# Turning activations by VectorE squares and DMAs instead of TensorE, in a two-layer hybrid decoder on one core

## What is computed

```
layer 0:  h += 0.5*SwiGLU(rms(h));  h += S5(rms(h));    h += 0.5*SwiGLU(rms(h))
          k, v = rms(h) @ w_kv
layer 1:  h += 0.5*SwiGLU(rms(h));  h += attn(rms(h));  h += 0.5*SwiGLU(rms(h))
out = rms(h)
swiglu(x) = (silu(x @ w_in[:, :F]) * (x @ w_in[:, F:])) @ w_out          # F = 2816
S5: 64 groups of 16 channels, 64 complex states each, a linear scan over time,
    then gelu, then (z @ w_glu[:, :1024]) * sigmoid(z @ w_glu[:, 1024:])
attn: 16 heads of 64, causal in the one block of 256 tokens, with a distance penalty
```

## Time and profile before

| | us |
|---|---|
| median of 3 runs | 972.12 (972.08 to 974.28) |
| profiled execution, its own time | 969.86 |
| its span, first to last instruction | 967.7 |
| TensorE busy | 955.9 |
| VectorE, ScalarE, GpSimd busy | 597.8, 499.8, 189.5 |

### The profile page before, as it was taken

How to read it: one execution, slowest core, us unless ns; L and a number is a source line. 1 busy time by engine, 2 the same in 40 slices (tenths; PEclk the granted TensorE clock), 3 DMA queues, 4 the chain that set the end, 5 groups by cost and what they waited for, 6 DMA issues and landing times.

```text
span 967.7 us, 15102 instructions
## 1 busy us (share of the span) xinstructions
PE 955.9 (99%) x6110; PEld 790.2 (82%) x6110; DVE 597.8 (62%) x744; ACT 499.8 (52%) x711; POOL 189.5 (20%) x235
## 2 busy tenths in 40 slices
PE   9999999999999999999999999999999999999997
PEld 7888888788788888888888888888888888888886
DVE  5565779889765554656555555555557555656544
ACT  7554544576555454545544454554458454545441
POOL 4899999800000000000000000000060000000000
PEclk9999999999999999999999999999999999999999
DMA  9766555520455655565566666656651366555551
GB/s 347 269 184 197 181 174 174 175 69 5 142 187 193 194 178 194 184 208 183 166 198 196 193 177 196 191 177 195 188 182 45 111 198 193 186 187 192 179 169 43
DMA packets 47557, 169.35 MB, mean 175 GB/s; under 512 B 5505, under 2 KB 5505, under 8 KB 47489
## 3 DMA queue, kind: packets, MB, share of 16 engines
q1 hardware_dynamic: 47056, 167.79, 54.5%
q10 hardware_dynamic: 432, 0.61, 0.2%
HBM read 167.33 MB, written 1.05 MB: 174 GB/s over the span
## 4 chain that ended last, share of the span: by engine, by line
PE 88%; DVE 8%; issue 2%; ACT 1%; DMA 1%; SPq 0%; POOLq 0%; POOL 0%; DVEq 0%; ACTq 0%
PE ps L1252 85%; DVE w_lo L931 2%; PE ps L1257 2%; DVE scan L1158 1%; DVE tmp L1087 1%; PE ps L1284 1%; DMA raw<-in_in 1%; DVE rot_b L1165 1%; DVE rot_a L1145 1%; DVE rot_b L1147 1%; ACT w_hi L652 0%; DVE rot_in L1154 0%; DVE states L1172 0%; PE ps L1297 0%; ACT pr L881 0%
## 5 line engine op out<-in xcount | busy, mean ns | idle before, releaser
L931 DVE TENSOR_TENSOR w_lo<-raw,w_hi 128x1024 fp32r<-128x1024 f32 x311 | 399.7, 1289 | 307.0 <-ACT w_hi L652 305.7
L652 ACT ACTIVATE w_hi<-raw 128x1024 fp32r<-128x1024 f32 x311 | 328.4, 1059 | 305.9 <-PE ps L1252 303.2
L1252 PE MATMUL ps<-w_hi,x_hi 128*128 128x512 f32 x896 | 352.4, 393 | 0.9 <-DVE w_lo L931 0.6
L1252 PE MATMUL ps<-w_hi,x_lo 128*128 128x512 f32 x896 | 349.3, 390 | 0.0
L1252 PE MATMUL ps<-w_lo,x_hi 128*128 128x512 f32 x896 | 349.2, 390 | 0.0
L1252 PEld LDWEIGHTS ps<-w_hi,x_hi 128*128 128x128 f32 x896 | 168.4, 188 | 37.2 <-DVE w_lo L931 1.4
L1252 PEld LDWEIGHTS ps<-w_hi,x_lo 128*128 128x128 f32 x896 | 168.3, 188 | 35.2
L1252 PEld LDWEIGHTS ps<-w_lo,x_hi 128*128 128x128 f32 x896 | 168.5, 188 | 34.0
L1252 PE MATMUL ps<-w_hi,hid_hi 128*128 128x512 f32 x352 | 138.1, 392 | 1.0 <-DVE w_lo L931 1.0
L1252 PE MATMUL ps<-w_lo,hid_hi 128*128 128x512 f32 x352 | 137.2, 390 | 0.0
L1252 PE MATMUL ps<-w_hi,hid_lo 128*128 128x512 f32 x352 | 137.2, 390 | 0.0
(11 more groups left out here) (151 smaller groups left out, 599.6 us busy)
## 6 DMA issues: line engine op xcount, KB each, us to landing
raw<-in_in SPq DMA_DIRECT2D x175, 512.0 KB, 4.3
raw<-in_out SPq DMA_DIRECT2D x88, 512.0 KB, 3.4
raw<-in_glu SPq DMA_DIRECT2D x16, 512.0 KB, 4.3
raw<-in_k SPq DMA_DIRECT2D x8, 512.0 KB, 4.4
raw<-in_v SPq DMA_DIRECT2D x8, 512.0 KB, 4.1
raw<-in_q SPq DMA_DIRECT2D x8, 512.0 KB, 4.4
raw<-in_o SPq DMA_DIRECT2D x8, 512.0 KB, 4.0
xt<-in_xt SPq DMA_DIRECT2D x4, 256.0 KB, 5.6
```

The source lines that it names most:

```text
L652: act.activation(w_hi[:, gu % WS, :], raw[:, gu % RAW, :], ACT.Copy)\
L931: dve.tensor_tensor(w_lo[:, gu % WS, :], raw[:, gu % RAW, :], w_hi[:, gu % WS, :].bitcast(F32), ALU.subtract)\
L1252: return pe.matmul(o, w, x, start=start, stop=stop, skip_group_check=True)
```

## The change

Three kinds of data are no longer turned by TensorE: the gated blocks of all four feed-forwards, the blocks of k and q, and those parts of h that are listed in `SHEETS` (GLU 0 to 2, and the first block of the outputs 4 and 8). `BY_ROWS` lists the nine parts of h that TensorE still turns.

In place of it VectorE transposes every square of 32 by 32 in itself (`dve.transpose`), gated blocks in place in `prod`, k, q and h into a new tile `sheet`. The squares then have to change places: square (q, c), of token group q and channel group c, goes to partitions 32c. SyncE does that with 16 DMAs per block, SBUF to SBUF, one for each (q, c), in pieces of 32 floats. They go to `hid_lo`, `x_lo`, `k_sb` or `q_sb`. ScalarE makes the high part of what has landed, and VectorE subtracts in place.

The moves stand in SyncE's queue behind the load of a fixed unit (8 units, `MOVE_BEHIND`, behind the block's end). Gated blocks are copied by ScalarE in unit 1 of the block after next, and finished by VectorE in unit 2. Parts of h from a sheet are read in unit 3 of the next block (GLU), or units 4 and 5 (outputs). q's scale moves into the norm's factor, one more small GpSimd instruction. There is one sheet, so a drain of k or q waits until the sheet before has been moved; `scores` waits for the move of its q block.

```diff
-BATCH = 4
-BATCHES = (0, 4, 8)
+SLOTS = 4
+SHEETS = [(2, 0), (2, 1), (2, 2), (4, 0), (5, 0), (5, 1), (8, 0), (9, 0), (9, 1)]
+BY_ROWS = [(2, 3), (4, 2), (4, 3), (8, 2), (8, 3), (10, 0), (10, 1), (10, 2), (10, 3)]
+MOVED = 16 * QS * QS
+MOVE_BEHIND = 8
...
 def high_behind(p, phases, b, j):
-    if p.name == "in" and b in BATCHES[1:] and j >= 2:
+    if p.name == "in" and b >= 2 and j == 1:
+        return [(p, b - 2)]
...
+        def pieces(g, q, c):
+            return prod_of(g)[Q * q:Q * q + Q].rearrange("p t (a c x) -> p c (t a) x", a=2, x=Q)[:, c]
+        def places(b, q, c):
+            return hid_lo[Q * c:Q * c + Q, 2 * b:2 * b + 2, :].bitcast(F32)\
+                .rearrange("p i (t q x) -> p q (i t) x", t=TT, x=Q)[:, q]
...
 @block.sync
+            def move_hidden(p, b):
+                g = p.hid0 + b
+                sp.wait_ge(hid_squares, g + 1)
+                for q in range(QS):
+                    for c in range(QS):
+                        sp.dma_start(places(b, q, c), pieces(g, q, c)).then_inc(hid_moved[g % SLOTS], 16)
...
             for gu in range(10, len(units)):
                 load(gu)
+                if gu in moves:
+                    move_hidden(*moves[gu])
+                if gu in sheet_moves:
+                    move_sheet(*sheet_moves[gu])
...
 @block.scalar
             def high_hidden(p, b):
-                act.wait_ge(hid_turned, p.hid0 + min(b // BATCH * BATCH + BATCH, p.blocks))
+                act.wait_ge(hid_moved[g % SLOTS], 16 * QS * QS * (g // SLOTS + 1))
...
+                if p.name == "glu" and j == (1 if (p.n, b) in BY_ROWS else 3):
                     high_x(p.n, b)
...
 @block.vector
+                if p.name == "in":
+                    dve.wait_ge(drained, p.drained0 + TT * (b + 1))
+                    whole = prod_of(p.hid0 + b).rearrange("p t x -> p (t x)")
+                    dve.transpose(whole, whole).then_inc(hid_squares, 1)
             def low_hidden(p, b):
-                dve.tensor_tensor(halves(hid_lo[:, 2 * b:2 * b + 2, :].rearrange("p f x -> p (f x)")),
-                                  turned_block(b),
...
+                part = hid_lo[:, 2 * b:2 * b + 2, :]
+                dve.tensor_tensor(part, part.bitcast(F32), hid_hi[:, 2 * b:2 * b + 2, :].bitcast(F32),
+                                  ALU.subtract).then_inc(hid_ready, 1)
+            def turned_h(p, b, w):
+                dve.wait_ge(drained, p.drained0 + TT * (b + 1))
+                dve.wait_ge(sheet_moved, MOVED * SHEETS.index((p.n, b)))
+                for q in range(TT):
+                    ins = dve.transpose(sheet[:, 0:w // P, q, :],
+                                        h[:, q, w * b:w * b + w].rearrange("p (i x) -> p i x", x=P))
...
 @block.tensor
             def scores(i):
-                pe.wait_ge(kq_ready, 4 + i // 2 + 1)
+                pe.wait_ge(sheet_moved, MOVED * (SHEETS.index((9, i // 4)) + 1))
```

More of the change, by code:

```diff
@@ L108, in follow_ups, with gate_unit, high_behind @@
     return [(phases[p.n - 1], phases[p.n - 1].blocks - 1, j)] if chained else []
[L111 to L115, removed]
-        f = phases[p.n - 1]
-        return f, range(BATCHES[-1], f.blocks)
-    return p, range(0)
-def high_behind(p, phases, b, j):
-    if p.name == "in" and b in BATCHES[1:] and j >= 2:
[L124 to L129, removed]
+def gate_unit(p, b):
+    return (b + 1) * p.upb + (2 if p.n == 0 and b == 0 else 0)
+def high_behind(p, phases, b, j):
+    if p.name == "in" and b >= 2 and j == 1:
+        return [(p, b - 2)]
+    if p.name == "out" and b == 0 and j in (1, 4):
+        f = phases[p.n - 1]
+        return [(f, f.blocks - 2 + j // 4)]
     return []
 def low_behind(p, phases, b, j):
[L135 to L140, removed]
+    if p.name == "in" and b >= 2 and j == 2:
+        return [(p, b - 2)]
+    if p.name == "out" and b == 0 and j in (2, 5):
+        f = phases[p.n - 1]
+        return [(f, f.blocks - 2 + j // 5)]
     return []
@@ L303, in trunk @@
         act_ready = sem("act_ready")
-        hid_turned = sem("hid_turned")
+        hid_squares = sem("hid_squares")
+        hid_moved = [sem(f"hid_moved{i}") for i in range(SLOTS)]
         hid_hi_done = sem("hid_hi_done")
@@ L391, in trunk @@
             sq_at[n] = total, parts
-        turned = {nc_: i for i, nc_ in enumerate((n, c) for n in (2, 4, 8, 10) for c in range(DT // 2))}
+        turned = {at: t for t, at in enumerate(BY_ROWS)}
         NORM = {0: 1, 3: 2, 5: 3, 6: 3, 7: 3, 9: 4, 11: 5}
@@ L694, in high_x @@
             def high_x(n, c):
-                act.wait_ge(h_turned, turned[n, c] + 1)
+                if (n, c) in BY_ROWS:
+                    act.wait_ge(h_turned, turned[n, c] + 1)
+                else:
+                    act.wait_ge(sheet_moved, MOVED * (sheet_of(n, c) + 1))
                 for gain, buf in X_OF[n]:
@@ L722, in after @@
                     squares(p, b, NB)
-                if p.n in (4, 8, 10) and j == 1:
-                    for c in (2 * b, 2 * b + 1):
-                        high_x(p.n, c)
+                if p.n in (4, 8, 10):
+                    for i in range(2):
+                        if j == (1 if (p.n, 2 * b + i) in BY_ROWS else 4 + i):
+                            high_x(p.n, 2 * b + i)
                 if p.name in ("k", "q") and j == 0:
@@ L1258, in turn @@
                 return last
-            def turn_hidden(f, batch):
-                if not batch:
-                    return
-                pe.wait_ge(drained, f.drained0 + TT * (batch[-1] + 1))
-                if f.hid0 + batch[0]:
-                    pe.wait_ge(hid_ready, f.hid0 + batch[0])
-                if f.n == 7 and batch[0] == 0:
-                    pe.wait_ge(kq_ready, 4)
-                for b in batch:
-                    for i in range(2):
-                        for q in range(TT):
-                            last = turn(KT + b % BATCH // 2 * 2, b % 2 * HB + (2 * i + q) * HP,
-                                        prod_of(b)[:, q, i * P:i * P + P])
-                    last.then_inc(hid_turned, 1)
             def turn_h(p, c):
                 t = turned[p.n, c]
-                if c >= 2 or p.n != 2:
-                    before = (p.n, c - 2) if c >= 2 else ({4: 2, 8: 4, 10: 8}[p.n], c + 2)
-                    pe.wait_ge(x_ready, bank_read[before])
+                if t >= 2:
+                    pe.wait_ge(x_ready, bank_read[BY_ROWS[t - 2]])
                 for i in range(2):
```

149 lines of the change are left out of this document (78 added, 71 removed).

## The result

The changed kernel takes 1077.26 us (median of 4 runs, 1071.39 to 1078.69), the kernel before on the same chip 973.2 (4 runs, 972.08 to 974.7): ratio 1.106, 95% interval 1.101 to 1.110. The forecast was 972.6 with a range of 961 to 988. One of the rivals came true in kind, the one in which SyncE's queue becomes the bound (chance 0.07); its 1034 us are still 43 short.

A forecast was written before the change was run, and what follows sets the result against it. TensorE was taken as the bound nearly everywhere. Savings of -15.3, shared read path +3.8, GLU +7.6 and attention +4.4 summed to +0.5 us, giving 972.6 us, range 961 to 988.

The forecast's parts named there:

- the one in which SyncE's queue becomes the bound: Rival: at 0.60 us per issue each of 44 gated blocks takes 12.0 us; 1034 us in all, chance 0.07.
- the price of one issue on SyncE's queue: In every move: 16 DMAs issued 0.42 us apart, the last landing 8.2 us after the first issue.
- Gated blocks: Four feed-forwards: moved blocks arrive in time, any landing up to 19.0 us costs nothing; 0 us.
- GLU: Parts of h in the GLU: moves land too late for ScalarE's x_hi, so TensorE waits; +7.6 us.
- The recurrence: In the GLU: each late landing delays the next block's squares; waits of 0.4 and 7.2 us, sum 7.6.
- attention: Scores 0 and 4 wait for the moves of q's blocks, 2.1 and 2.3 us; +4.4 us.
- the misread row of scores 4: In attention: scores 4 taken to stand at 737.8 us, q's second block landing at 740.1; a wait of 2.3 us.
- The shared read path: Before the state-space stage: VectorE's subtraction from two SBUF operands stretches GpSimd's chain up to `cp`; +3.8 us.
- What is saved: TensorE's turns dropped in feed-forwards, h, k and q: 18.5 us, of which 15.3 kept; 3.20 per feed-forward.
- The small pieces: Rival: moves' 128-byte pieces choke the DMA engines in each of 44 blocks; some 1160 us, chance 0.04.

The follow-up runs named there:

- e7: Kernel before plus 8 unused transfers per gated block in the last three feed-forwards, SBUF to SBUF, six forms by turns: 970.3 us, one run.
- e10: Kernel before plus 8 unused transfers per gated block in the last three feed-forwards, three forms, source by turns SBUF or HBM: 972.8 us, one run.
- e1: Changed kernel with only gated blocks moved; h, k and q turned by TensorE as before: 1036.1 us, ratio 1.067 to the kernel before.
- e3: Changed kernel with two gated blocks moved by one set of 16 transfers: 1002.2 us, ratio 1.031 to the kernel before.
- e5: Changed kernel with gated blocks' moves in the last three feed-forwards issued by GpSimd, not SyncE: 1019.9 us, ratio 1.048.
- e2: Changed kernel with only h, k and q moved, by sheets; gated blocks turned by TensorE as before: 1008.1 us, ratio 1.038.
- e9: Changed kernel with sheets only, each sheet's 16 transfers issued half by SyncE, half by GpSimd: 982.2 us, ratio 1.011.
- e8: Changed kernel, gated blocks moved in pairs in last three feed-forwards, k and two parts of h by sheets, the rest by TensorE: 956.6 us, ratio 0.985.
- e11: Kernel before plus 16 unused transfers per gated block in the last three feed-forwards, read from HBM: 971.9 us, ratio 1.000.
- e12: Kernel before plus 12 unused SBUF-to-SBUF transfers per gated block in the last three feed-forwards: 971.8 us, ratio 1.000.

## Why the prediction was wrong, point by point

**The failed step: the price of one issue on SyncE's queue.** I took 0.42 us for a move's issue from a median of 0.327 and a pitch of 0.47 at the start. Both rows are loads from HBM, and the first are mostly single ones behind a wait. Back to back such transfers do cost 0.43; moves from SBUF cost 0.60 (e7, e10), at a pitch of 0.64. So the queue needed 12.3 us and more for a block of 10.94, where I had 8.4. The rival that used 0.60 was given 0.07, and nothing in the trace of before spoke against it: the maximum of the row was 0.655, and no row showed a transfer between two places of SBUF. It was a resource at 8.4 of 10.94 us by a guessed price, and the threshold stood at 0.547, inside the ends that I had named for the price elsewhere (0.33 to 0.65). The same price went into three terms.

**Gated blocks: forecast 0, measured +65.8** (e1), and less than nothing once the queue is relieved (phases 7 and 11: -2.8 in e3, -2.0 and -2.4 in e5). I had room for a landing up to 19.0 us behind the block's end, but the sets start 12.8 us apart in e1 and the blocks end 10.94 apart, so the room is soon gone; from there on ScalarE waits for every block. Ten intervals of 1.9 less 3.2 of turns are 15 us, as measured in the last three feed-forwards. The rival had 12.0 us per block at 0.60; it forgot the 0.04 between issues and the loads' 0.5, which make 12.3, and the slow issues, which make 12.9. For attention it had half of what was measured. The two terms are 40 of the 43 us that it fell short. The first feed-forward loses more (20 us), and even with pairs 6.5, beside GpSimd (e3).

**GLU: forecast +7.6, measured +18.8** (e2). The recurrence was right. Squares were ready 5.5 us after each landing. With a move of 15 x 0.64 + 1.9 = 11.5 in place of 8.2 it gives landings at 14.2 and 20.3, a third at 26.4, and the fourth part's gating at 31.2, where TensorE wants it at 14.1: 17.1. The term was mis-sized by the price. A smaller part is the clock again: TensorE waited 1.4, 0.5, 5.1 and 8.0 us, 15.0 in all, and behind the last two its matmuls started 0.43 us apart for a while in place of 0.23, which cost 3.3. For e9 the recurrence gives 5.4 with 7.6 for every move, and 5.8 was measured, but that is partly luck: only the first of the three moves took 7.7, the others 6.3, and TensorE waited 3.6.

**Attention: forecast +4.4, measured +20.0** (e2). The waits were put in the right two places. The price adds 3.6 to each, the misread row of scores 4 adds 2.9 to the second: 5.7 and 8.8; measured 5.6 and 9.1. What I had not counted at all is the clock. From scores 0 until TensorE wanted scores 4, e2 needed 2.9 us more than the kernel before, most of it in the 28 matmuls above. Behind the second stall it runs 9.5 us to where the kernel before, at full clock, needs 5.9. Waits 14.7 and slow clock 2.9 + 3.6 make 21.2; less the last turn, 0.9, 20.3.

**The shared read path: forecast +3.8, measured about +1.0.** In e3, GpSimd ends the last `cp` (start us, us) at 179.69, before at 178.69:

```profile
177.54 2.15 POOL L621 TENSOR_TENSOR cp<-tmp 128x512 f32<-128x512 f32 x1
```

The stretch was real but fell on VectorE. Its subtraction in the changed kernel before 140 us, and after 350, when GpSimd is idle (ns min/median/max):

```profile
L1046 DVE TENSOR_TENSOR hid_lo<-hid_lo,hid_hi x8: 682/1544/1801, 44.4 to 133.5; 128x512 fp32r<-128x512 f32 x8
...
L1046 DVE TENSOR_TENSOR hid_lo<-hid_lo,hid_hi x9: 682/684/686, 355.1 to 458.2; 128x512 fp32r<-128x512 f32 x9
```

In the changed kernel `cp` even ended at 170.57, with TensorE so late that nobody waited for it. I had put the stretch at 0.43 us on GpSimd's chain, and expected about 1.0 for the subtraction; it took 0.86 more than alone, and GpSimd's chain hardly any. The trace of before had shown VectorE's side: `w_lo`, 1.23 us alone, took up to 2.1 beside GpSimd, for example here.

```profile
142.72 1.97 DVE L931 TENSOR_TENSOR w_lo<-raw,w_hi 128x1024 fp32r<-128x1024 f32 x1
```

**What is saved: right, a little low.** e8 saves 2.8 us in each of three feed-forwards and 1.1 in the output behind it (2.0 where a sheet of h adds 0.9): 3.9 where I had 3.2. The transposes took 0.712 and 1.25 us for 0.7 and 1.3, a sheet's landings 1.84 to 1.93 for 1.9, but a gated block's moves landed after 2.4 in the median. The small pieces did not fill the DMA engines; that `raw` landed later than before (5.5 us for 4.3) cost nothing in e11 and e12, where it was 4.8 and 4.9.

## What to carry to other kernels

A queue is an engine: count its issues per block, and price one of the same kind, back to back, before calling it free. Where the trace has no such row, reckon with the price's upper end. If the price at which the queue becomes the bound lies inside the ends that you allow for it, this rival is no rarity. Many small transfers are merged (here two blocks to one set) or spread over queues that have room; making each smaller gains nothing.

## What the runs showed of the hardware

A transfer into SBUF costs SyncE's queue, back to back, 0.59 to 0.64 us when read from SBUF, for 32, 64 or 128 rows, 1 to 8 pieces per row and 4 to 32 KB (e3, e7, e10), and 0.42 to 0.43 when read from HBM, for 32 or 128 rows, 1 or 4 pieces and 16 or 32 KB (e10, e11). GpSimd's issue costs 0.55; its moves landed after 3.3 us in the median of e5 and after 1.9 in e9. TensorE's clock was granted at 0.50 to 0.62 behind stalls of 5.6 and 9.1 us (e2), so a stall cost about 1.4 times its own length there.
